# A first layer norm applied on the transposed side: weight and bias per partition, chunk by chunk

## The reference

```python
h = _layer_norm(x, ln_in_g, ln_in_b)          # (x - mean) * rsqrt(var + eps) * g + b
z = h @ w_in[i]                               # 1024 -> 1280 = pool channels | q | k | v
y_pool = _pool_mixer(z[..., :s_q], pool_w[i], pool_scale[i])
y_attn = _window_attention(z[..., s_q:s_k], z[..., s_k:s_v], z[..., s_v:], attn_sinks[i])
mix = jnp.concatenate([y_pool, y_attn], axis=-1) @ w_o[i]
h = _layer_norm(DEEPNORM_ALPHA * h + mix, ln1_g[i], ln1_b[i])
```

## Time and profile before

| | us |
|---|---|
| median of 3 runs | 1427.75 (1427.12 to 1431.62) |
| the profiled execution, its own time | 1432.45 |
| its span | 1430.4 |
| PE busy | 1346.9 (94%) |
| DVE busy | 1178.2 (82%) |
| ACT busy | 660.5 (46%) |
| POOL busy | 538.9 (38%) |
| PE on the chain that ended last | 69% |

### The profile page before, as it was taken

The page is one execution under the profiler, slowest core; times in us unless marked ns, Lnnn a source line. Parts: engine busy times, 40 slices in busy tenths (PEclk is TensorE's granted clock), DMA queues, the critical chain, the costliest instruction groups (busy, mean ns, idle before and its releaser), DMA issues.

```text
span 1430.4 us, 23303 instructions
## 1 busy us (share of the span) xinstructions
PE 1346.9 (94%) x7689; PEld 726.2 (51%) x7689; DVE 1178.2 (82%) x2324; ACT 660.5 (46%) x908; POOL 538.9 (38%) x346
## 2 busy tenths in 40 slices
PE   2998989999997999999979999999998999999994
PEld 2454445545664666666635555555553444444441
DVE  6353639999999799999867877878888889888888
ACT  3452345555666666676623343333433333333332
POOL 1131113344554533333334445455655443232221
PEclk9997999999998999999989999999999999999997
DMA  7221232233663899999889999999999999999971
GB/s 298 68 74 47 72 103 77 89 114 111 182 185 119 281 371 368 365 362 355 336 287 332 329 335 330 330 322 369 366 372 338 372 391 392 382 375 370 367 263 64
DMA packets 147209, 381.32 MB, mean 267 GB/s; under 512 B 11600, under 2 KB 70224, under 8 KB 144976
## 3 DMA queue, kind: packets, MB, share of 16 engines
q1 hardware_dynamic: 110288, 246.38, 48.9%
q0 software_dynamic: 36864, 134.23, 25.4%
HBM read 339.15 MB, written 41.42 MB: 266 GB/s over the span
## 4 chain that ended last, share of the span: by engine, by line
PE 69%; DVE 21%; issue 4%; DMA 3%; ACT 2%; POOL 0%; DVEq 0%; SPq 0%; ACTq 0%; POOLq 0%
PE bank L572 33%; PE bank L561 9%; PE bank L563 9%; PE bank L562 9%; DVE area L1313 2%; DVE area L1305 2%; DVE area L1307 2%; DMA ple_sb<-v_rows_dram,expert_id 2%; DVE area L1343 2%; DVE area L1302 2%; DVE area L1310 1%; PE bank L589 1%; PE bank L764 1%; PE bank L766 1%; DVE area L1317 1%
## 5 line engine op out<-in xcount | busy, mean ns | idle before, releaser
L572 PE MATMUL bank<-cut,area 128*128 128x512 f16 x2328 | 517.0, 382 | 14.9 <-DVE area L1495 9.7
L561 PE MATMUL bank<-hT,cut 128*128 128x384 f16 (+1 forms) x1232 | 415.0, 337 | 16.5 <-ACT gelu_out L1006 7.8
L563 PE MATMUL bank<-hT,cut 128*128 128x384 f16 (+1 forms) x1232 | 414.9, 337 | 0.0
L562 PE MATMUL bank<-hT,cut 128*128 128x384 f16 (+1 forms) x1232 | 414.9, 337 | 0.0
L572 PEld LDWEIGHTS bank<-cut,area 128*128 128x128 f16 x2328 | 229.0, 98 | 291.7 <-issue 13.7
L1123 DVE SCALAR_TENSOR_TENSOR cut<-raw,cut 128x1024 f16<-128x1024 f32 x242 | 295.5, 1222 | 84.3 <-ACT cut L823 82.7
L823 ACT ACTIVATE cut<-raw 128x1024 f16<-128x1024 f32 x242 | 250.4, 1053 | 199.3 <-PE bank L572 168.6
L523 POOL DMA_INDIRECT ple_sb<-u_rows_dram,expert_id x128 | 199.9, 1562 | 290.0 <-DVE dots_now L1416 279.7
L523 POOL DMA_INDIRECT ple_sb<-v_rows_dram,expert_id x128 | 170.0, 1328 | 258.6 <-DVE ple_gate L1507 244.6
L513 POOL TENSOR_TENSOR cut<-raw,cut 128x1024 f16<-128x1024 f32 x56 | 126.7, 2264 | 168.0 <-ACT cut L833 167.9
L1006 ACT ACTIVATE gelu_out<-bank 128x384 f32<-128x384 f32 x120 | 58.7, 489 | 269.7 <-PE bank L563 269.7
(11 more groups left out here) (131 smaller groups left out, 1144.9 us busy)
## 6 DMA issues: line engine op xcount, KB each, us to landing
raw<-tiles_dram SPq DMA_DIRECT2D x298, 512.0 KB, 5.9
gates_scratch<-area SPq DMA_DIRECT2D x12, 2048.0 KB, 11.9
area<-gates_scratch SPq DMA_DIRECT2D x32, 768.0 KB, 8.8
gelu_scratch<-gelu_out SPq DMA_DIRECT2D x72, 192.0 KB, 4.5
area<-gelu_scratch SPq DMA_DIRECT2D x18, 768.0 KB, 10.6
norm_rows<-norms_dram SPq DMA_DIRECT2D x3, 1024.0 KB, 8.5
hn<-x_dram SPq DMA_DIRECT2D x4, 512.0 KB, 5.2
ple_sb<-u_rows_dram,expert_id POOLq DMA_INDIRECT x128, 8.1
```

The costliest lines, as they stand in the source:

```text
L561: nc.tensor.matmul(dst, w[0], hT[:, 0, k, 0:width], start=(k == 0), stop=False)
L562: nc.tensor.matmul(dst, w[0], hT[:, 1, k, 0:width], start=False, stop=False)
L563: last = nc.tensor.matmul(dst, w[1], hT[:, 0, k, 0:width], start=False, stop=(k == KD - 1))
L572: mm = nc.tensor.matmul(bank[:, 2 * tt + h, :], lhs(a)[:, tt * P:(tt + 1) * P], cut[:, t.slot, b, h * HALF:(h + 1) * HALF], start=(first a ...
```

## The change

The weight and the bias of the first layer norm are no longer applied to the rows that are transposed. The rows are only centred and scaled, then transposed; in the banks a feature is a partition, so the weight and bias are one scalar each per partition. They come in 16 new columns of `small` (`gain_cols`).

```diff
-POOL_ADDS = ((0, 2), (0, 1, 2), (0, 1, 2))
+POOL_ADDS = ((), (0, 1, 2), (0, 1, 2))
-    return i % 4 if stage else i
+    return i % 4 if stage else (0, 1, 2, 3, 5, 6, 7, 0)[i]
+        gain_cols = small_sb[:, 8 + GROUPS + GROUPS * PAD:].rearrange("p (w k) -> p w k", w=2)
+        x_turned = ple_sb
 # SP
-            load_norms(0)
             sp.dma_start(ident_sb[:], ident).then_inc(ident_in, 16)
+            sp.dma_start(small_sb[:], small).then_inc(small_in, 16)
             load(Tile(0)); load(Tile(1)); load(Tile(2))
             sp.dma_start(alibi_sb, alibi).then_inc(consts_in, 16)
-            sp.dma_start(small_sb[:], small).then_inc(consts_in, 16)
             sp.dma_start(pool_w_sb, pool_w).then_inc(consts_in, 16)
             load(Tile(3))
+            load_norms(0)
...
-            load_norms(1)
             for n in range(4, T_Q + RING):
+                if n == T_O + 4:
+                    load_norms(1)
                 load(Tile(n))
 # POOL
-            add_b(0)
+            pool.wait_ge(norms_in, 16)
+            pool.wait_ge(turned_lo, KD)
+            for t in range(TT):
+                nc.gpsimd.tensor_tensor(hn[:, t, :], hn[:, t, :], norm_rows[:, 0, :], ALU.mult).then_inc(rows_scaled, 1)
+                pool.wait_ge(rows_scaled, t + 1)
+                nc.gpsimd.tensor_tensor(hn[:, t, :], hn[:, t, :], norm_rows[:, 1, :], ALU.add).then_inc(norm_done, 1)
 # PE
+            def turn_columns():
+                pe.wait_ge(centred, TT)
+                for k in range(KD):
+                    if k == KD - 1:
+                        pe.wait_ge(gained_by_dve, 1)
+                    for t in range(TT):
+                        last = nc.tensor.transpose(bank[:, turn_bank(0, k), t * P:(t + 1) * P],
+                                                   hn[:, t, k * P:(k + 1) * P], ident_sb[:])
+                    last.then_inc(turned, 1)
...
                 for k in range(KD):
+                    if as_turned:
+                        pe.wait_ge(turned_lo, k + 1)
...
-            turn(0)
-            pe.wait_ge(turned_lo, KD)
+            turn_columns()
+            columns(Tile(0), 0, 0, as_turned=True)
...
-            for n in range(3):
+            for n in range(1, 3):
 # ACT
-                for m in mine:
+                for m in mine if stage else range(2):
...
+            def gain(k):
+                act.wait_ge(turned, k + 1)
+                nc.scalar.activation(x_turned[:, k, :], bank[:, turn_bank(0, k), :], ACT.Identity,
+                                     bias=gain_cols[:, 1, k:k + 1],
+                                     scale=gain_cols[:, 0, k:k + 1]).then_inc(gained_by_act, 1)
+            def gained_hi(k):
+                act.wait_ge(gained_by_act if k % 2 else gained_by_dve, k // 2 + 1)
+                nc.scalar.activation(hT[:, 0, k, :], x_turned[:, k, :], ACT.Copy, scale=S_ACT).then_inc(turned_hi, 1)
             roots(0)
             split_hi(Tile(0))
+            act.wait_ge(small_in, 16)
+            gain(1); gained_hi(0); gain(3); gained_hi(1); gained_hi(2); gain(5)
+            gained_hi(3); gained_hi(4); gain(7); gained_hi(5); gained_hi(6); gained_hi(7)
             split_hi(Tile(1))
-            turn_hi(0)
 # DVE
-            for i in range(TT):
-                layer_norm(0, i)
-            for i in (1, 3):
-                add_b(0, i)
+            dve.wait_ge(shift_done, 1)
+            for t in range(2, TT):
+                nc.vector.tensor_scalar(hn[:, t, :], hn[:, t, :], rstd[:, t:t + 1], shift[:, t:t + 1], ALU.mult,
+                                        ALU.add).then_inc(centred, 1)
             split_lo(Tile(0))
+            def gain(k):
+                dve.wait_ge(turned, k + 1)
+                nc.vector.tensor_scalar(x_turned[:, k, :], bank[:, turn_bank(0, k), :], gain_cols[:, 0, k:k + 1],
+                                        gain_cols[:, 1, k:k + 1], ALU.mult, ALU.add).then_inc(gained_by_dve, 1)
+            def gained_lo(k):
+                dve.wait_ge(turned_hi, k + 1)
+                nc.vector.scalar_tensor_tensor(out=hT[:, 1, k, :], in0=x_turned[:, k, :], scalar=S_ACT,
+                                               in1=hT[:, 0, k, :], op0=ALU.mult, op1=ALU.subtract).then_inc(turned_lo, 1)
+            dve.wait_ge(small_in, 16)
+            gain(0); gain(2); gained_lo(0); gained_lo(1); gain(4); gained_lo(2)
+            gained_lo(3); gain(6); gained_lo(4); gained_lo(5); gained_lo(6); gained_lo(7)
             split_lo(Tile(1))
-            turn_lo(0)
...
+                dve.wait_ge(norm_done, t + 1)      # before each residual sum
```

More of the change, by code:

```diff
@@ L193, in layer @@
         pool_scale_s = sb("pool_scale_s", [P, GROUPS])
-        small_sb = sb("small_sb", [P, 8 + GROUPS + GROUPS * PAD])
+        small_sb = sb("small_sb", [P, 8 + GROUPS + GROUPS * PAD + 2 * KD])
         sink = small_sb[:, 0:8]
         pool_scale = small_sb[:, 8:8 + GROUPS]
-        inv_count = small_sb[:, 8 + GROUPS:].rearrange("p (g t) -> p g t", g=GROUPS)
+        inv_count = small_sb[:, 8 + GROUPS:8 + GROUPS + GROUPS * PAD].rearrange("p (g t) -> p g t", g=GROUPS)
+        gain_cols = small_sb[:, 8 + GROUPS + GROUPS * PAD:].rearrange("p (w k) -> p w k", w=2)
         ident_sb = sb("ident_sb", [P, P])
@@ L290, in layer @@
         weight_cut = part([RING, 2, TD], F16)
-        ident_in, consts_in, tables_in, ple_loaded, subkeys_in, norms_in = (sem(n) for n in (
-            "ident_in", "consts_in", "tables_in", "ple_loaded", "subkeys_in", "norms_in"))
+        ident_in, small_in, consts_in, tables_in, ple_loaded, subkeys_in, norms_in = (sem(n) for n in (
+            "ident_in", "small_in", "consts_in", "tables_in", "ple_loaded", "subkeys_in", "norms_in"))
         x_in = [sem(f"x_in{t}") for t in range(TT)]
@@ L302, in layer @@
         turned, turned_hi, turned_lo = sem("turned"), sem("turned_hi"), sem("turned_lo")
+        gained_by_dve, gained_by_act = sem("gained_by_dve"), sem("gained_by_act")
         pads_zero, v_turned, v_band_done = sem("pads_zero"), sem("v_turned"), sem("v_band_done")
@@ L479, in add_b @@
                     nc.gpsimd.tensor_tensor(rows_t, rows_t, norm_rows[:, 1, :], ALU.add).then_inc(done, 1)
-            add_b(0)
+            pool.wait_ge(norms_in, 16)
[4 more added lines that the diff above has]
+                nc.gpsimd.tensor_tensor(hn[:, t, :], hn[:, t, :], norm_rows[:, 1, :], ALU.add).then_inc(norm_done, 1)
             pool.wait_ge(pads_zero, 3)
-            pool.wait_ge(consts_in, 16 * 3)
+            pool.wait_ge(consts_in, 16 * 2)
             for g in range(GROUPS):
@@ L552, in turn, with columns @@
                     last.then_inc(turned, 1)
-            def columns(t, index, parity, width=T, first_bank=4):
+            def turn_columns():
[7 more added lines that the diff above has]
+                    last.then_inc(turned, 1)
+            def columns(t, index, parity, width=T, first_bank=4, as_turned=False):
                 pe.wait_ge(lo_cut, t.n + 1)
@@ L646, in _ @@
             pe.wait_ge(ident_in, 16)
-            turn(0)
-            pe.wait_ge(turned_lo, KD)
+            turn_columns()
+            columns(Tile(0), 0, 0, as_turned=True)
             pe.wait_ge(pads_zero, 3)
-            pe.wait_ge(consts_in, 16 * 3)
-            for n in range(3):
+            pe.wait_ge(consts_in, 16 * 2)
+            pe.wait_ge(small_in, 16)
+            for n in range(1, 3):
                 columns(Tile(n), n, n % 2)
@@ L891, in take_y @@
                                      scale=pool_scale_s[:, g:g + 1]).then_inc(y_hi, 1)
+            def gain(k):
[6 more added lines that the diff above has]
+                nc.scalar.activation(hT[:, 0, k, :], x_turned[:, k, :], ACT.Copy, scale=S_ACT).then_inc(turned_hi, 1)
             roots(0)
             split_hi(Tile(0))
+            act.wait_ge(small_in, 16)
+            gain(1)
+            gained_hi(0)
+            gain(3)
+            gained_hi(1)
+            gained_hi(2)
+            gain(5)
+            gained_hi(3)
+            gained_hi(4)
+            gain(7)
+            gained_hi(5)
+            gained_hi(6)
+            gained_hi(7)
             split_hi(Tile(1))
-            turn_hi(0)
             act.wait_ge(pads_zero, 3)
-            act.wait_ge(consts_in, 16 * 3)
+            act.wait_ge(consts_in, 16 * 2)
             split_hi(Tile(2))
@@ L1220, in _ @@
             row_moments(0, EPS)
-            for i in range(TT):
-                layer_norm(0, i)
-            for i in (1, 3):
-                add_b(0, i)
+            dve.wait_ge(shift_done, 1)
+            for t in range(2, TT):
+                nc.vector.tensor_scalar(hn[:, t, :], hn[:, t, :], rstd[:, t:t + 1], shift[:, t:t + 1], ALU.mult,
+                                        ALU.add).then_inc(centred, 1)
             split_lo(Tile(0))
+            def gain(k):
[7 more added lines that the diff above has]
+            dve.wait_ge(small_in, 16)
+            gain(0)
+            gain(2)
+            gained_lo(0)
```

(14 more changed lines are left out.)

## The result

The changed kernel takes 1416.09 us (median of 4 runs, 1414.08 to 1418.29) against 1429.68 (4 runs, 1427.12 to 1432.47) before: ratio 0.9903, 95% interval 0.9881 to 0.9926, 13.6 us less. The forecast was 1414.1, the range 1411.5 to 1418.5. The profiled execution took 1415.96 us, its span 1414.1.

A forecast was written before the change was run, and what follows sets the result against it. Everything up to the first column matmul bounds the end one for one, then PE to 104 us. Terms 7.1, 2.6 and 4.0 make 13.7 us off the median 1427.75: 1414.1 us, range 1411.5 to 1418.5.

The forecast's parts named there:

- The mark: Start of column tile 1's first matmul on PE: forecast at 26.8 us instead of 40.54, gain 13.7 us.
- low 1: DVE's low part (subtraction) of transposed chunk 1, forecast to end at 20.8 us.
- low 7: DVE's last low part, of chunk 7, forecast to end at 25.6 us (bounds 25.0 and 27.6).
- DVE's gain: DVE's weight-and-bias operation on a transposed chunk from a bank: taken as 0.69 us, bounds 0.60 and 0.75.
- 2.6 is tile 0 at full clock: Term of the gain: column tile 0's matmuls take 5.2 us at full clock instead of 7.8, worth 2.6 us.
- 4.0 is tile 0 beside the chain: Term of the gain: tile 0's 5.2 us run beside the low-part chain, 1.2 staying behind it, worth 4.0 us.
- the earlier last low part: Term of the gain: the last low part is ready at 25.6 us instead of 32.7, worth 7.1 us.
- rival A: PE's clock still low when tile 0 starts: tile 1 at 29.7, gain 10.0 to 11.7, time 1416.8 us; chance 0.14.
- rival B: Dearer hand-overs, or POOL before DVE's split of tile 1: gain 10.0 to 12.0, time 1416.7 us; chance 0.13.
- rival C: POOL's eight operations delay nine long DVE operations, 2.17 us each: 5.8 us slower, 1433.5 us; chance 0.03.
- rival D: Gain vanishes in PE's waits at 104 to 127 us if something there had a fixed time; chance 0.04.
- The covers: Moved POOL work and loads stay hidden: POOL ends at 44.5 to 51.8 us; moving norm rows 1 brings no gain.

The follow-up runs named there:

- e1: Changed kernel, but PE waits for all eight low parts before column tile 0, as before the change: 1423.66 us, ratio to before 0.9945.
- e2: As e1, plus 44 further PE transposes of the identity between the turning and that wait: 1423.16 us, ratio to before 0.9933.
- after: The changed kernel as first measured and profiled, against the kernel before the change: 1416.09 us, ratio 0.9903.
- e6: Kernel before the change, with weight and bias applied to only one column of each row tile: 1422.46 us, ratio to before 0.9951.
- r11: The changed kernel measured again, unaltered, 6 runs: 1415.73 us, ratio to before 0.9894.
- e5: Changed kernel, but norm rows 0 are loaded right behind x, as before the change: 1414.70 us, ratio to before 0.9894.
- e3: Changed kernel, but POOL applies weight and bias to only one column of each residual row tile: 1416.72 us, ratio to before 0.9895.
- e9: Changed kernel, plus 22 PE transposes of the identity ahead of the turning: 1416.41 us, ratio to before 0.9917.
- e4: Changed kernel, but the load of norm rows 1 stays ahead of tile 4 on the SP queue: 1436.27 us, ratio to before 1.0035.
- e7: Changed kernel, but ACT splits tile 0 before the square root: 1418.38 us, ratio to before 0.9931.
- e10: Changed kernel with ACT's split of tile 0 between square root and centrings, plus the 22 transposes of e9: 1412.01 us, again 1413.96.

## Why the prediction was right

*The mark.* Forecast 14.35 us from shift to tile 1 (26.8 - 12.45), measured 14.75; the gain 13.7, measured 13.3 in the trace and 13.6 in the medians. The transposes start 2.71 us after the shift (forecast 2.65), low 1 ends at 8.42 (8.35), low 3 at 10.34 (10.15), low 7 at 13.47 (13.15), and tile 1 follows 1.28 later (1.2). Of the 0.4 us in all, 0.25 arise between low 1 and low 7, where two of DVE's gains stand between low parts. The term that was mis-sized is DVE's gain. Durations in ns (min/median/max) in the changed kernel:

```profile
L1268 DVE TENSOR_SCALAR hn<-hn,rstd,shift x2: 804/809/814, 13.2 to 14.0; 128x1024 f32<-128x1024 f32 x2
...
L1274 DVE TENSOR_SCALAR ple_sb<-bank,small_sb x4: 800/804/811, 17.7 to 23.3; 128x512 f32<-128x512 f32 x4
L1279 DVE SCALAR_TENSOR_TENSOR hT<-ple_sb,hT x8: 676/680/693, 19.3 to 25.8; 128x512 f16<-128x512 f32 x8
...
L918 ACT ACTIVATE ple_sb<-bank,small_sb x4: 766/773/779, 17.8 to 22.9; 128x512 f32<-128x512 f32 x4
L924 ACT ACTIVATE hT<-ple_sb x8: 613/622/631, 18.6 to 24.7; 128x512 f16<-128x512 f32 x8
```

DVE's gain from the bank is 0.80, above my upper bound of 0.75: I had taken the price of an operation with one scalar per partition, and this one has two; whether that makes the difference no run shows. The same operation on twice the columns in SBUF, the centring, takes 0.81: that form is cheap there, 1.53 us for two rows against my bound of 2.4, and it changed nothing, since ACT ended at 15.6. ACT's terms, 0.77 and 0.62 against 0.75 and 0.60, were right.

*The decomposition.* "2.6 is tile 0 at full clock" measured 2.5 (e1 less e2), "4.0 is tile 0 beside the chain" measured 3.97 (e2 less after). What remains of the 13.3, 6.9, is the earlier last low part, forecast 7.1. The last low part comes 20.27 us after the shift before, 12.95 in e6, where the old layout has the gain for nothing, and 13.47 here. So taking the weight and bias off the rows is enough for all of it, and the new order by itself loses 0.5. That 0.5 is a net: gains in the banks on both engines, against two centrings fewer on ACT and a weight split moved behind the chain on each; no run takes these apart. The 5.1 us between e6 and the changed kernel are the overlap and the clock, less that 0.5. The clock counts for less there than in e1, since e6's tile 0 takes 6.84 us and e1's 7.66.

*Where it was luck.* The 1414.1 stood on a median before of 1427.75 from three runs. With the fourth it is 1429.68, and from there the same 13.7 gives 1416.0; 1416.09 was measured. But the medians of the changed kernel and of before differ by 13.6 here and by 15.8 in r11, by 14.6 in e5 and 14.3 in e3, which are the same kernel but for details without effect on the time. So that 13.6 meets 13.7 to a tenth is chance. These differences lie on the whole above the 13.3 of the trace. A microsecond more behind the first w_o tile, like the 1.4 of the clock above, would fit, but with one profile of before it is not shown. For the profiled execution the sum said 1418.75, and it took 1415.96.

*The clock (rival A).* Wrong. The transposes of the changed kernel, first stretch and last:

```profile
L570 PE MATMUL bank<-ident_sb,hn x11: 421/421/448, 15.7 to 17.9; 128*128 128x128 f32 x11
...
L570 PE MATMUL bank<-ident_sb,hn x11: 272/273/351, 20.3 to 21.4; 128*128 128x128 f32 x11
```

They fall from 421 to 273 ns among themselves, with nothing but transposes on PE since the start, and e2 and e9 show the same two ways. The Trainium skill, "TensorE: Matmul & The Clock Gate", Part 4: PE-mode transpose, states that the full rate doesn't engage for transposes; here it does, and the measurement decides. The granted clock in the records reads 1.00 all along in this stretch, so only the durations tell it.

*POOL first (rival B).* Wrong (and its upper gain of 12.0 didn't follow from its own 29.2 for tile 1, which makes 11.3). DVE's split began at 26.42, before POOL was released at 26.65, and POOL got its turn only after the second split as well: its first multiply shows 4.34 us, of which 2.35 is work. The Trainium skill, "SBUF — State Buffer", Who interferes with whom, says that whichever of the two starts first holds the shared ports for the whole instruction; the trace agrees, and adds that an instruction right behind it on DVE went ahead of the waiting POOL too.

*POOL starves DVE (rival C).* The holding is about as priced, 3.14 us once for a split (3.38 forecast) and 2.3 for small operations, yet PE waited 0.3 us in all; e3 puts its cost at nothing that can be measured.

*Given back (rival D).* Not: 23.3 us of pooling stretch in both.

*The covers.* POOL ended at 50.5 (bounds 44.5 to 51.8), small landed at 10.2, norm rows 0 at 19.7 (I said 19). The weak point of my text is the move of norm rows 1: I priced what the move costs, not what staying would have cost, and so didn't say that the change depends on it. e4 says it: 20 us.

## What to carry to other kernels

When a vector is applied along the free axis before a transpose, apply it behind the transpose as a scalar per partition; and look as well for what this allows, the consumer starting chunk by chunk while its engine stays warm: it was half of the gain here (6.4 of 13.3 us). When work moves behind the critical path, follow every load that waits for its semaphore: one load left in its old place turned 13 us of gain into 5 of loss. To judge an edit of 1 us in a run that scatters by 5, measure between two marks of the trace that lie around it. Here they repeat to 0.01 us in most profiles (14.74 to 14.75 in after, r11, e4, e5 and e7), but e3 shows a chance difference of 0.28; so see first whether the stretch up to the edit is alike.

## What I had not expected of the hardware

- Transposes alone raised and held PE's clock: 44 of them in a gap of 5 us kept it at 1.00 (e2), 22 on the identity made the next 32 take 3.71 instead of 5.95 us (e10).
- DVE's TENSOR_SCALAR with two scalars per partition takes 0.80 us on 512 columns from a bank and 0.81 on 1024 in SBUF; the SCALAR_TENSOR_TENSOR beside it 0.68 on 512.
- A four-column TENSOR_SCALAR on DVE took 2.32 us beside POOL, and 0.17 without it (e3).
- A split moved ahead of ACT's square root put a second table load (1.28 us) between the two, on the path; the one in the idle start stayed (e7).
- The landing of x scatters: without e7, whose root was late, the shift began between 11.45 and 13.03 us over 13 profiles, with x ahead of everything on its queue.
